# Summing the two halves of a low-rank projection before the gates, first score level on quadrants, and another load order in the opening

## What is computed

```python
sh1, sc1, ... = ada_mod(cond, w_ada, b_ada)            # silu(cond) @ w_ada, two conditions
h = rmsnorm(x, g_mix) * (1 + sc1) + sh1
gq, gk, gv, gr, zf, zb, nq, nk, nv, m_gla, m_na = split_in(h @ w_in)
la_f = log_sigmoid(zf @ w_af + b_af) / 16              # zf, zb: 16 columns each
la_b = log_sigmoid(zb @ w_ab + b_ab) / 16
o_gla, s_f, s_b = gla_bidir(q, k, v, la_f, la_b, s0_f, s0_b)   # chunked gated linear attention
o_na = na_latent_attention(qn, kn, vn, k_ctx, v_ctx, rpb)      # k_ctx: the cached keys
```

## Time and profile before

| what | value |
|---|---|
| median of 3 timed runs | 969.75 us (969.64 to 969.89) |
| profiled execution | 970.44 us |
| its span in the profile | 968.6 us |
| PE busy | 952.3 us of 968.6 |
| DVE, POOL, ACT busy | 603.2, 503.9, 434.7 us |

### The profile page before, as it was taken

One profiled execution on the slowest core, in us unless ns is written; L12 is line 12 of the kernel. 1 busy time (PEld: TensorE's weight loads), 2 busy tenths in 40 slices (PEclk: granted clock), 3 DMA queues, 4 the chain that ended last, 5 costly groups with the idle time before them and its releaser, 6 DMA issues.

```text
span 968.6 us, 18808 instructions
## 1 busy us (share of the span) xinstructions
PE 952.3 (98%) x7513; PEld 866.9 (89%) x7513; DVE 603.2 (62%) x1087; ACT 434.7 (45%) x683; POOL 503.9 (52%) x361
## 2 busy tenths in 40 slices
PE   6999999999999999999999999999999999999998
PEld 5799899977888899999987999999999999888886
DVE  6508359963575769434937998777777778903002
ACT  5244165523766564342404465555555556511110
POOL 1386723323332317772724378888888885433331
PEclk9999999999999999999999999999999999999999
DMA  9896222126011133888641313222222222322331
GB/s 335 270 157 97 78 76 55 58 77 185 23 30 38 45 86 100 265 251 296 236 152 44 88 45 87 88 86 84 82 83 82 83 83 72 121 81 82 105 107 55
DMA packets 127826, 108.20 MB, mean 112 GB/s; under 512 B 8342, under 2 KB 104571, under 8 KB 127483
## 3 DMA queue, kind: packets, MB, share of 16 engines
q1 hardware_dynamic: 122728, 99.81, 34.1%
q0 software_dynamic: 1696, 3.25, 2.3%
q10 hardware_dynamic: 3315, 3.94, 1.1%
HBM read 101.45 MB, written 4.47 MB: 109 GB/s over the span
## 4 chain that ended last, share of the span: by engine, by line
PE 87%; DVE 5%; SPq 2%; issue 2%; POOL 1%; ACT 1%; DMA 1%; DVEq 0%; POOLq 0%; ACTq 0%
PE PA L1649 6%; PE PA L1647 6%; PE PA L1648 6%; PE PJ L923 6%; PE PJ L928 5%; PE PJ L924 5%; PE PA L1533 3%; PE PA L1535 3%; PE PA L1534 3%; PE PJ L1533 3%; PE PJ L1535 3%; PE PJ L1534 3%; PE PJ L1441 2%; PE PA L1367 2%; PE PJ L1442 2%
## 5 line engine op out<-in xcount | busy, mean ns | idle before, releaser
L713 POOL TENSOR_TENSOR wlo<-wraw,whi 128x1024 fp32r<-128x1024 f32 x53 | 133.1, 2513 | 257.4 <-ACT whi L1704 167.4
L923 PE MATMUL PJ<-h_hi,whi 128*128 128x320 f32 x336 | 104.8, 320 | 0.1
L924 PE MATMUL PJ<-h_lo,whi 128*128 128x320 f32 x336 | 101.1, 309 | 0.0
L928 PE MATMUL PJ<-h_hi,wlo 128*128 128x320 f32 x336 | 76.5, 309 | 0.0
L1704 ACT ACTIVATE whi<-wraw 128x1024 fp32r<-128x1024 f32 x39 | 41.0, 1052 | 71.8 <-PE PJ L928 23.2
L923 PEld LDWEIGHTS PJ<-h_hi,whi 128*128 128x128 f32 x336 | 63.0, 188 | 5.8 <-issue 3.6
L2220 ACT ACTIVATE whi<-wraw 128x1024 fp32r<-128x1024 f32 x21 | 22.3, 1060 | 98.6 <-PE PA L1535 51.6
L924 PEld LDWEIGHTS PJ<-h_lo,whi 128*128 128x128 f32 x336 | 63.1, 188 | 0.0
L880 POOL TENSOR_TENSOR behind<-behind_val,behind 128x512 fp32r<-128x512 f32 x40 | 52.0, 1301 | 19.0 <-ACT behind L2199 19.0
L1649 PE MATMUL PA<-h_hi,behind 128*128 128x320 f32 x192 | 59.3, 309 | 0.0
L928 PEld LDWEIGHTS PJ<-h_hi,wlo 128*128 128x128 f32 x336 | 56.1, 188 | 0.0
(11 more groups left out here) (593 smaller groups left out, 3234.3 us busy)
## 6 DMA issues: line engine op xcount, KB each, us to landing
wraw<-in_w_in_dram SPq DMA_DIRECT2D x72, 256.0 KB, 3.2
ada_rest<-in_w_ada_dram SPq DMA_DIRECT2D x32, 512.0 KB, 6.1
wraw<-in_w_up_dram SPq DMA_DIRECT2D x48, 256.0 KB, 3.8
wraw<-in_w_down_dram SPq DMA_DIRECT2D x42, 256.0 KB, 3.0
raw_even<-in_w_up_dram SPq DMA_DIRECT2D x40, 256.0 KB, 3.6
ada<-in_w_ada_dram SPq DMA_DIRECT2D x16, 512.0 KB, 7.5
out_dram<-x ACTq DMA_DIRECT2D x10, 256.0 KB, 2.1
x_rows<-in_x_sample_dram SPq DMA_DIRECT2D x2, 1024.0 KB, 6.5
```

The costliest lines, as they stand in the source:

```text
L713: pool.tensor_tensor(wlo[:, slot, 0:k, :], wraw[:, slot, 0:k, :], whi[:, slot, 0:k, :].bitcast(F32), ALU.subtract).then_inc(lo_done, done)
L923: pe.matmul(out, whi[:, slot, w0 + k, :], hi(k)[:, tok], start=start and k == k0, stop=False)
L924: pe.matmul(out, whi[:, slot, w0 + k, :], lo(k)[:, tok], start=False, stop=False)
L928: mm = pe.matmul(out, wlo[:, slot, w0 + k, :], hi(k)[:, tok], start=False, stop=stop and k == k1 - 1)
```

## The change

Five edits, in the order of the program:

1. PE starts with four transposes of the identity into columns of `PA` that the level-0 copies read but nothing else has written.
2. SP issues `w_z` and `ada_half(1, 1)` ahead of the second `w_in` chunk.
3. PE runs `low_rank(g)` ahead of `modulation_rows(g + 1, 1)`.
4. `low_rank` puts its sums at groups `b + 2 * (k % 2)`; ACT makes three copies in place of one (z, and the two halves crossed into `la_e`), DVE adds them, so each 32-row group of z holds whole sums of one token half; each gate product contracts 32 rows on a row group of its own. `gate_pair(0)` waits for the addition.
5. The key transposes go through `by_rows` (16 of 64 rows), with a copy that reads them so; level 0 takes the quadrant form of the others.

```diff
@@ SP
-            chunk(0, 0, w_in_v, P, None)
-            ada_half(1, 1)
             sp.wait_ge(tab_in, 16)
             sp.dma_start(w_z[:, :, :], w_in_v[:, :, IN_Z:IN_Z + 32]).then_inc(tab_in, 16)
+            ada_half(1, 1)
+            chunk(0, 0, w_in_v, P, None)
@@ PE
             pe.wait_ge(tab_in, 16)
+            for at_ in (1344, 1408, 1856, 1920):
+                unread(1, at_)
             pe.wait_ge(cvec_in, 16 * 3)
...
-                        c0 = 32 * (2 * b + k % 2)
+                        c0 = 32 * (b + 2 * (k % 2))
...
+                low_rank(g)
                 if g < ADA_GROUPS - 1:
                     modulation_rows(g + 1, 1)
-                low_rank(g)
...
-                    tr = pe.transpose(PA[:, j * PAST + b * P:j * PAST + (b + 1) * P], kc_tok[:, b, j * P:(j + 1) * P], ident[:, :])
+                    tr = by_rows(lambda i: psum("PA", i), (2 * j + b) * 64, kc_tok[:, b, j * P:(j + 1) * P])
...
+                else:
+                    pe.wait_ge(z_made, ADA_GROUPS + 1)
                 for m in range(2):
                     for b in range(2):
+                        c0 = 32 * (2 * m + b)
                         mm = pe.matmul(PA[:, m * 1024 + b * BANK:m * 1024 + b * BANK + HALF],
-                                       w_alpha[64 * b:64 * b + 64, 2 * d + m, :], z[64 * b:64 * b + 64, :], start=True, stop=True)
+                                       w_alpha[c0:c0 + 32, 2 * d + m, :], z[c0:c0 + 32, :], start=True, stop=True)
...
-                            for h in range(2 if n else 1):
+                            for h in range(2):
                                 for r in range(2):
-                                    at_, m = 64 * h, 64 if n else P
+                                    at_, m = 64 * h, 64
@@ ACT
-            act.activation(z[:, :], PJ[:, 0:HALF], ACT.Copy).then_inc(tile_freed, 1)
+            act.activation(z[:, :], PJ[:, 0:HALF], ACT.Copy)
+            act.activation(la_e[0:64, 0, 0:HALF], PJ[64:128, 0:HALF], ACT.Copy)
+            act.activation(la_e[64:128, 0, 0:HALF], PJ[0:64, 0:HALF], ACT.Copy).then_inc(tile_freed, 1)
@@ DVE
+            dve.wait_ge(tile_freed, 2)
+            dve.tensor_tensor(z[:, :], z[:, :], la_e[:, 0, 0:HALF], ALU.add).then_inc(z_made, 1)
             dve.wait_ge(hlo_set, NK)
```

More of the change, by code:

```diff
@@ L413, in hybrid_dit_step @@
         past_in, mask_in = sem("past_in"), sem("mask_in")
-        z_ps = sem("z_ps")
+        z_made = sem("z_made")
         rpb_in = sem("rpb_in")
@@ L1014, in low_rank @@
                     for b in range(2):
-                        c0 = 32 * (2 * b + k % 2)
+                        c0 = 32 * (b + 2 * (k % 2))
                         mm = pe.matmul(PJ[c0:c0 + 32, 0:HALF], w_z[:, k, :], h_t[:, k % 4, b * HALF:(b + 1) * HALF],
                                        start=g == 0, stop=g == ADA_GROUPS - 1)
-                mm.then_inc(z_ps, 1)
+                mm.then_inc(z_made, 1)
             for t in range(3):
@@ L1785, in _ @@
             act.wait_ge(tile_ready, 2)
-            act.wait_ge(z_ps, ADA_GROUPS)
-            act.activation(z[:, :], PJ[:, 0:HALF], ACT.Copy).then_inc(tile_freed, 1)
+            act.wait_ge(z_made, ADA_GROUPS)
+            act.activation(z[:, :], PJ[:, 0:HALF], ACT.Copy)
+            act.activation(la_e[0:64, 0, 0:HALF], PJ[64:128, 0:HALF], ACT.Copy)
+            act.activation(la_e[64:128, 0, 0:HALF], PJ[0:64, 0:HALF], ACT.Copy).then_inc(tile_freed, 1)
             for n in (2, 3, 4, 5):
@@ L1792, in _ @@
                     act.wait_ge(kct_ps, 1)
-                    act.activation(kcT[:, :, :].rearrange("p a b -> p (a b)"), PA[:, 0:1024], ACT.Copy).then_inc(kct_cp, 1)
+                    act.activation(kcT[:, :, :].rearrange("p j (b i n) -> p (j b) i n", i=2, n=64), from_halves(PA[:, 0:1024]), ACT.Copy)\
+                   .then_inc(kct_cp, 1)
                 if n >= 4:
@@ L2393, in _ @@
                         dve.wait_ge(hlo_set, k - 3)
-                        dve.wait_ge(z_ps, g - 1)
+                        dve.wait_ge(z_made, g - 1)
                     for r, cols in enumerate((slice(0, SAMPLE), slice(SAMPLE, TOK))):
```

## The result

| | median | lowest to highest | executions |
|---|---|---|---|
| before | 969.92 us | 969.57 to 971.64 | 9 |
| changed | 972.61 us | 969.88 to 973.68 | 9 |

The recorded ratio of the executions is 1.0018, with a 95% interval of 1.0009 to 1.0026: a little slower, by some 1.7 us. It is not the ratio of the two medians, which stand 2.7 us apart; so 1.7 to 2.7 us is what the nine executions of each support. The executions of the changed kernel spread over 3.8 us, and the mean granted clock that each reports goes with it: the one of 969.88 us reports 1.000, the eight from 971.57 us up report 0.996 to 0.998. The profiled execution has a span of 971.1 us and a clock of 0.998; that of before had 968.6.

A forecast was written before the change was run, and what follows sets the result against it. PE's own work was taken to bound the kernel, loads its opening. Savings of 2.3 us against losses of 2.1 and 0.9 gave +0.7 us: 970.5 us median from 969.75, range 967.7 to 972.5.

The forecast's parts named there:

- The case called likeliest: Whole kernel: savings and losses nearly cancel, forecast with its spread, 968.8 to 971.8 us, chance 0.54.
- the clock: Rival, opening: PE's rest of over 3 us halves TensorE's pace for 3 us, costing 1.5 us, 972.0 us; chance 0.22.
- PE's list decides, opening delays are paid in full: Whole span: PE hardly waits behind the opening, so savings behind 48 us and delays in the opening count in full.
- Gates, 1.06 us: Gate products on PE: two pairs go from 1.28 to 0.75 us each, saving 1.06 us, 0.9 to 1.3.
- Level 0, 1.05 us: Level 0 on PE: quadrant form takes level 1's 1.32 us instead of 2.44; saves 1.05 us, 1.0 to 1.12.
- Keys, 0.2 us: Key transposes on PE: through `by_rows` 0.71 us instead of 1.04; saving taken as 0.2 us, 0.1 to 0.33.
- Hidden additions: Added start transposes, ACT copies and DVE addition: hidden in idle time; addition done about 48.5 us, `gate_pair(0)` at 63.4.
- The late chunk, 2.1 us: Opening: second chunk lands at 27.0 us instead of 23.1, delaying DVE's row copy and PE by 2.1 us, 1.0 to 3.0.
- thin stretch of transfers: Opening loads: 309 GB/s instead of 371 from 24 to 31 us, over 1 us of transfer, so a later chunk landing.
- The gaps in groups 1 and 2, 0.9 us: PE's new order: PE stands still 0.47 us per group during DVE's modulation-row copy; 0.9 us, 0.7 to 1.0.
- A new stall behind the gates: Rival at `project(1, 6)`: PE, 0.7 us sooner, may wait for POOL's low part; up to 0.5 us, put inside the forecast.

The follow-up runs named there:

- e5: The kernel before with only the new opening (new load order, low-rank products ahead of modulation products): 973.76 us against 970.39, ratio 1.0033.
- e8: The changed kernel plus one wait: DVE's five down-projection subtractions start only when POOL has finished its fifth chunk; 971.43 us against 970.39 before, ratio 1.0009.
- e3: The changed kernel with only PE's old order put back, loads in the new order: 971.55 us against 971.40 for the kernel before, ratio 1.0002.
- e6: The changed kernel with the old opening put back and one DVE wait for POOL in the down projection: 968.09 us against 970.39 before, ratio 0.9974.
- e9: The kernel of e8 with 10 unread identity transposes in PE's rest before group 1's turn to columns: 970.25 us against 970.97 before, ratio 0.9984.

## Why the prediction was right, and where it was off

The range of 967.7 to 972.5 holds 969.75 x 1.0018 = 971.5 us, and the sign within it, a little up, is that of the sum; the median itself, 972.61, lies 0.1 beyond its upper end. The case called likeliest was not what happened most, and that the number came out so near is in part luck. The sum's own terms, as measured, give -2.1 + 1.1 + 0.9 = -0.1 us instead of +0.7. What carried the kernel above the one before was the clock, the rival that was given 0.22, and a stall that no step had.

- **PE's list decides, opening delays are paid in full.** Right. The distance of 3.4 us at the end of the opening stayed until the savings took their share, and e5 has it at the end, beside the 1.1 us of the stall.
- **Gates, 1.06 us.** Right: two times 1.28 to 0.75, and 1.05 on the distance between the traces. The row of line 1240 was the same shape and gave the number to 0.01 us.
- **Level 0, 1.05 us.** Right: 1.03 by the distance.
- **Keys, 0.2 us.** Mis-sized: 0.02. The prediction named the effect (what follows overlaps differently) and still took most of the difference of busy times. The row of the first product behind was what was missing.
- **Hidden additions.** Right. The three copies and the addition ended at about 52 us, fifteen before `gate_pair(0)`.
- **The late chunk, 2.1 us.** The mechanism step by step as forecast (chunk, high part, low part, row copy, turn to columns); the term mis-sized: the turn to columns came at 28.66 instead of 27.38, 1.28 later, of which 0.26 is the wait for `ada` that it replaces; and together with the two gaps the opening cost 2.0 us where the clock held (e8). By both this term is 1.0 to 1.1. The step that failed is the landing: 26.1 us, which both of the readings in the prediction gave (26.3 from bytes, 26.4 from the place in the queue). The 0.6 us more for the thin stretch of transfers was wrong: in the changed kernel the rate from 24 to 30 us is 364 to 384 GB/s.
- **The gaps in groups 1 and 2, 0.9 us.** Right: two waits of 0.41 us in PE's timeline, 0.5 us each with the step to the copy; e3 has none of them. What was said beside it, that the new order on PE fills the 0.87 us wait for `ada`, was wrong: e3 has the old order on PE and no such wait, so it is the load order that takes it away.
- **The clock.** The mechanism, its price (1.5 us forecast; 1.3 to 1.4 between groups, 1.5 in the profile) and its place were right, the chance of 0.22 was far off. It fell in eight of nine executions of the changed kernel, in five of eight of e5, in six of eleven of e8 and e3. A rest of 2.4 us, shorter than the 3.3 us forecast, is enough more often than not. With it the sum of the profile is +3.4 - 2.1 = +1.3.
- **"A new stall behind the gates".** It didn't come; PE has no wait there. A stall of 1.1 us came 700 us further on, between POOL and DVE, which no step of the prediction looked at, as the edits don't touch that stage.

In sum: +2.0 opening, +1.4 clock, -2.1 savings, +1.1 stall where it occurs. The version that beats both is e6, the gates, keys and level 0 of the changed kernel with the old opening and one wait on DVE: 968.09 us against 970.39, ratio 0.9974 (0.9963 to 0.9984).

## What to carry to other kernels

Moving a load forward moves others back: follow the one that loses its place to the engine that handles it, and ask what else stands behind it in that engine's list. A rest of TensorE in the middle of a busy stretch is to be priced twice, for its length and for the clock behind it, and idle products that nobody reads can be the cheaper way. Work that fills the time of somebody else's copy is free only where it stands.

## What the runs showed of the hardware

- A rest of 2.4 to 2.5 us brought TensorE's granted clock to 1.2 GHz in 8 of 9, 5 of 8, 6 of 11 and 6 of 11 executions of four kernels, one of 1.6 us behind ten transposes in 1 of 11; twenty transposes in its place, in 0 of 22. In the three profiles that show it (changed, e5, e9) it came 0.5 to 1.5 us after the work had resumed, stayed from 30.2 to 33.6 us in the changed kernel, and cost 1.3 to 1.5 us.
- The record shows 1.00 at the start of the span, where the identity transposes run at half pace; in the middle the record and the pace agree.
- One subtraction on GpSimd took 2.7 or 6.4 us in the same program text, by whether it or five subtractions of VectorE beside it went through first; the loser took about the time of both.
- Products on quadrants or row groups are followed by a first whole product that takes 0.34 to 0.41 us on the chain (behind the groups at 66.86 and 138.22 us in the changed kernel and at 63.44 in the one before); behind the whole key transposes of the kernel before it takes 0.15.
